# Four of ten projection units reload raw weights and are rounded again by ScalarE in the latent blocks

## The reference, cut to what matters

```python
h = _rmsnorm(x, norm_mix_g) * (1.0 + sc1) + sh1
proj = jnp.einsum('btd,dc->btc', h, w_in)          # d = 1024, c = 2592
q, k, v, r, zf, zb, ga, gg = jnp.split(proj, [...], axis=-1)
gf = jax.nn.log_sigmoid((zf @ w_decay_f + b_decay_f)) / GATE_TAU
u = ga * jax.nn.sigmoid(gg)                        # then a 31-tap depthwise convolution
```

## Time and profile before

| | |
|---|---|
| Time before, median of 3 runs | 2376.88 us (2376.43 to 2378.6) |
| The profiled execution's own time | 2378.99 us |
| Its span, first to last instruction | 2377.3 us |
| Mean granted TensorE clock | 0.971 |
| PE busy / DVE busy / ACT busy / POOL busy | 94% / 70% / 50% / 30% |
| First stage: prompt, then blocks 0 to 3 | to about 145 us, then 145-291, 291-432, 432-572, 572-703 |

### The profile page before, as it was taken

One profiled execution on the slowest core, in us unless ns is written; L12 is line 12 of the kernel. 1 busy time (PEld: TensorE's weight loads), 2 busy tenths in 40 slices (PEclk: granted clock), 3 DMA queues, 4 the chain that ended last, 5 costly groups with the idle time before them and its releaser, 6 DMA issues.

```text
span 2377.3 us, 43867 instructions
## 1 busy us (share of the span) xinstructions
PE 2223.5 (94%) x16695; PEld 2050.0 (86%) x16695; DVE 1667.2 (70%) x2949; ACT 1195.1 (50%) x1939; POOL 704.5 (30%) x652
## 2 busy tenths in 40 slices
PE   4889999999998899976999999999999999999995
PEld 4778888898885577744999999999999999999995
DVE  2889989898898766667666656666566656666585
ACT  3765473644444455424545554455545554455573
POOL 4000000000000011101355445544555455534441
PEclk8999999999998899987999999999999999999998
DMA  8986677757847655354576677766776677766986
GB/s 297 342 312 212 232 254 242 249 199 262 241 147 232 203 197 191 106 168 117 190 210 193 183 200 200 203 197 177 202 214 192 179 200 202 203 192 184 300 251 239
DMA packets 290437, 505.79 MB, mean 213 GB/s; under 512 B 26193, under 2 KB 233934, under 8 KB 274704
## 3 DMA queue, kind: packets, MB, share of 16 engines
q1 hardware_dynamic: 250406, 376.39, 48.3%
q0 software_dynamic: 39424, 126.64, 19.6%
q10 hardware_dynamic: 490, 1.16, 0.1%
HBM read 405.61 MB, written 98.53 MB: 212 GB/s over the span
## 4 chain that ended last, share of the span: by engine, by line
PE 61%; DVE 4%; DMA 2%; ACT 1%; issue 1%; POOL 0%; SPq 0%; DVEq 0%; ACTq 0%; POOLq 0%
PE bank L1700 19%; PE bank L1702 19%; PE bank L1701 19%; PE bank L1954 1%; PE bank L2052 1%; DMA out_dram<-work_exp 1%; DVE work_exp L3063 1%; DVE work_proj L2654 1%; PE bank L1985 1%; DMA work_exp<-x_rows 0%; PE bank L2234 0%; DMA park_c<-work_proj 0%; DMA work_out<-park_c 0%; DVE work_out L2778 0%; PE bank L2061 0%
## 5 line engine op out<-in xcount | busy, mean ns | idle before, releaser
L1700 PE MATMUL bank<-act_hl_exp,hl_exp 128*128 128x288 f32 x3072 | 911.2, 297 | 11.7 <-DVE hl_exp L3242 7.7
L1701 PE MATMUL bank<-act_hl_exp,hl_exp 128*128 128x288 f32 x3072 | 908.9, 296 | 0.0
L1702 PE MATMUL bank<-act_hl_exp,hl_exp 128*128 128x288 f32 x3072 | 907.3, 295 | 0.0
L1700 PEld LDWEIGHTS bank<-act_hl_exp,hl_exp 128*128 128x128 f32 x3072 | 578.5, 188 | 12.7 <-DVE hl_exp L3242 9.2
L1702 PEld LDWEIGHTS bank<-act_hl_exp,hl_exp 128*128 128x128 f32 x3072 | 580.5, 189 | 0.0
L1701 PEld LDWEIGHTS bank<-act_hl_exp,hl_exp 128*128 128x128 f32 x3072 | 579.0, 188 | 0.0
L3242 DVE TENSOR_TENSOR hl_exp<-work_exp,hl_exp 128x1024 fp32r<-128x1024 f32 x192 | 231.4, 1227 | 206.4 <-ACT hl_exp L1283 206.4
L3242 DVE TENSOR_TENSOR hl_exp<-raw_exp,hl_exp 128x1024 fp32r<-128x1024 f32 x192 | 232.1, 1225 | 193.0 <-ACT hl_exp L1283 193.0
L2654 DVE SCALAR_TENSOR_TENSOR work_proj<-work_proj,wcv 128x392 f32<-128x392 f32 (+12 forms) x600 | 338.9, 635 | 1.2
L1283 ACT ACTIVATE hl_exp<-work_exp 128x1024 fp32r<-128x1024 f32 x192 | 199.3, 1055 | 201.3 <-PE bank L1702 201.1
L1283 ACT ACTIVATE hl_exp<-raw_exp 128x1024 fp32r<-128x1024 f32 x192 | 198.5, 1052 | 161.2 <-PE bank L1702 161.2
(11 more groups left out here) (425 smaller groups left out, 3288.8 us busy)
## 6 DMA issues: line engine op xcount, KB each, us to landing
hl_proj<-park_w POOLq DMA_DIRECT2D x80, 1024.0 KB, 6.4
raw_exp<-in_w_e_gate_dram SPq DMA_DIRECT2D x32, 1024.0 KB, 5.9
raw_exp<-in_w_e_up_dram SPq DMA_DIRECT2D x32, 1024.0 KB, 5.9
work_exp<-in_w_e_gate_dram SPq DMA_DIRECT2D x32, 1024.0 KB
work_exp<-in_w_e_up_dram SPq DMA_DIRECT2D x32, 1024.0 KB, 6.0
raw_exp<-in_w_e_down_dram SPq DMA_DIRECT2D x32, 1024.0 KB, 6.0
work_exp<-in_w_e_down_dram SPq DMA_DIRECT2D x32, 1024.0 KB, 6.1
park_w<-hl_proj SPq DMA_DIRECT2D x8, 2048.0 KB, 12.2
```

Source lines behind the costliest of these rows:

```text
L1700: pe.matmul(out, lh, rh, start=first, stop=False)
L1701: pe.matmul(out, lh, rl, start=False, stop=False)
L1702: return pe.matmul(out, ll, rh, start=False, stop=last_)
```

## The change

For units 2, 3, 4 and 5 (`ROUNDED`), three things change.

- The prompt stores only their low parts: 1 MB instead of 2 MB for each.
- In latent blocks POOL issues two transfers for each half: the raw weights (512 KB) from `w_in` into the place of the high part, and the low part (512 KB) from `park_w`. Both count on the same semaphore. A row of `w_in` has 2592 columns, so the raw half comes in runs of 128 floats (512 bytes), eight for each partition.
- ScalarE waits for both transfers, rounds the raw half in place (`round_half`, 128x1024) and raises `s_rnd`, and TensorE waits for `s_rnd` instead of the load. There are 8 such instructions in each latent block, 32 in all.

```diff
+        ROUNDED = (2, 3, 4, 5)
...
                     if j + 2 < NPROJ:
                         load_proj(j + 2)
-                    if SLOT[j] < 2:
+                    if j not in ROUNDED:
                         sp.dma_start(park_w[j], hl[:, SLOT[j]].bitcast(f32)).then_inc(s_stored[SLOT[j]], 16)
                         return
+                    if SLOT[j] < 2:
+                        sp.dma_start(park_w[j, :, :, 1], hl[:, SLOT[j], :, 1].bitcast(f32)).then_inc(s_stored[SLOT[j]], 16)
+                        return
                     for q in range(2):
-                        for i in range(2):
-                            sp.dma_start(park_w[j, :, q, i], w_part(b, j, q, i).bitcast(f32)).then_inc(s_wst2, 16)
+                        sp.dma_start(park_w[j, :, q, 1], w_part(b, j, q, 1).bitcast(f32)).then_inc(s_wst2, 16)
...
+            def round_half(b, j, q):
+
+                if b.prompt:
+                    return
+                b.wait(act, s_w[j % 2][q], loads_in(j))
+                act.activation(hl[:, j % 2, q, 0], hl[:, j % 2, q, 0].bitcast(f32), ACT.Copy).then_inc(s_rnd.sem, 1)
...
+                round_half(b, 2, 0)
                 sigmoid(b, 1, 0)
...
                 act.activation(W2["B"][:, 0:H * T], W2["B"][:, 0:H * T], ACT.Ln, bias=1.0).then_inc(s_ln.sem, 1)
+                round_half(b, 2, 1)
                 sigmoid(b, 1, 1)
                 proj_hi(b, 3)
                 for q in range(2):
                     copies(b, 2, q, "k", 1.0, s_kfb)
+                    round_half(b, 3, q)
...
                 for q in range(2):
                     copies(b, 3, q, "q", DK ** -0.5, s_qfb)
+                round_half(b, 5, 0)
...
             def load_w(b, j, q):
+                if j in ROUNDED:
+                    o = PROJ_COLS[j] + 128 * q
+                    pool.dma_start(hl[:, j % 2, q, 0], w_in_v[:, :, o:o + 128]).then_inc(s_w[j % 2][q].sem, 16)
+                    pool.dma_start(hl[:, j % 2, q, 1], park_w[j, :, q, 1]).then_inc(s_w[j % 2][q].sem, 16)
+                    return
                 pool.dma_start(hl[:, j % 2, q], park_w[j, :, q]).then_inc(s_w[j % 2][q].sem, 16)
...
                 if b.prompt:
                     pe.wait_ge(s_lo[s], 2 * (j // 2) + q + 1)
+                elif j in ROUNDED:
+                    b.wait(pe, s_rnd, 2 * (j - ROUNDED[0]) + q + 1)
                 else:
-                    b.wait(pe, s_w[s][q], 16 * (j // 2 + 1))
+                    b.wait(pe, s_w[s][q], loads_in(j))
```

More of the change, by code:

```diff
@@ L358, in hybrid_layer @@
         s_wst = [sem("s_wst0"), sem("s_wst1")]
-        s_w = [[sig(f"s_w{i}{q}", 0, 16 * (NPROJ // 2)) for q in range(2)] for i in range(2)]
+        s_w = [[sig(f"s_w{i}{q}", 0, 16 * (NPROJ // 2 + 2)) for q in range(2)] for i in range(2)]
         s_uh = sig("s_uh", 2 * NPROJ + 1, 2 * NPROJ + 1)
@@ L402, in hybrid_layer @@
         r_lt, r_co = s_pf.again(0), s_pb.again(0)
+        s_rnd = Sig(s_col, 0, 8, 2)
         r_wo = [Sig(s_m1[i], 0, 0, 16) for i in range(4)]
@@ L445, in hybrid_layer @@
         s_stored = [*s_wst, s_wst2]
-        f_x = [Sig(s_wst2, 0, 0, 16 * 8), Sig(sem("f_x1"), 0), Sig(k_T, 0, 0, 2), Sig(k_e, 0, 0, 1)]
+        f_x = [Sig(s_wst2, 0, 0, 16 * 4), Sig(sem("f_x1"), 0), Sig(k_T, 0, 0, 2), Sig(k_e, 0, 0, 1)]
         f_st = [Sig(s_vec2, 0, 0, 16), Sig(sem("f_st1"), 0)]
@@ L495, in turn, with loads_in @@
             return (base + j) // 2 + (per // 2) * i if not isinstance(i, int) or i else (base + j) // 2
-        SLOT, SLOT_TURN = (0, 1, 2, 0, 1, 2, 0, 1, 0, 1), (1, 1, 4, 2, 2, 8, 3, 3, 4, 4)
+        SLOT, SLOT_TURN = (0, 1, 2, 0, 1, 2, 0, 1, 0, 1), (1, 1, 2, 2, 2, 4, 3, 3, 4, 4)
+        ROUNDED = (2, 3, 4, 5)
+        def loads_in(j):
+            return 16 * sum(2 if i in ROUNDED else 1 for i in range(j % 2, j + 1, 2))
         SLOT_BEFORE = {j: max(i for i in range(j) if SLOT[i] == SLOT[j]) for j in range(3, NPROJ)}
@@ L958, in stage2 @@
                     modulate(nb, 0)
+                    round_half(b, 4, 0)
+                    round_half(b, 4, 1)
                 b.wait(act, s_cum, 2)
@@ L964, in stage2 @@
                                ACT.Exp, scale=1.0 / TAU).then_inc(s_D.sem, 1)
+                if b.i > 0:
+                    round_half(b, 4, 0)
                 b.wait(act, s_cl, 3)
@@ L1004, in latent_rest @@
                     modulate(nb, 1)
+                round_half(b, 5, 1)
+                if nb is not None:
                     modulate(nb, 2)
@@ L1726, in value_half @@
                 elif q == 0:
-                    b.wait(pe, s_w[s][0], 16 * (j // 2 + 1))
-                    b.wait(pe, s_w[s][1], 16 * (j // 2 + 1))
+                    b.wait(pe, s_w[s][0], loads_in(j))
+                    b.wait(pe, s_w[s][1], loads_in(j))
                 value_tile(b, j, 2 * q)
@@ L1850, in latent_rest @@
                     mod_pair(b, 0)
-                b.wait(pe, s_w[0][0], 16 * 5)
+                b.wait(pe, s_w[0][0], loads_in(8))
                 b.wait(pe, s_v, 1)
@@ L1857, in latent_rest @@
                 proj_part(b, 8, 0, 4, KC, 0, b.T).then_inc(s_uh.sem, 1)
-                b.wait(pe, s_w[0][1], 16 * 5)
+                b.wait(pe, s_w[0][1], loads_in(8))
                 b.wait(pe, s_v, 3)
@@ L1862, in latent_rest @@
                 proj_part(b, 8, 1, 4, KC, 0, b.T).then_inc(s_uh.sem, 1)
-                b.wait(pe, s_w[1][0], 16 * 5)
+                b.wait(pe, s_w[1][0], loads_in(9))
                 b.wait(pe, s_v, 2)
@@ L1870, in latent_rest @@
                     mod_pair(b, 1)
-                b.wait(pe, s_w[1][1], 16 * 5)
+                b.wait(pe, s_w[1][1], loads_in(9))
                 b.wait(pe, s_v, 4)
```

## The result

| | before | after |
|---|---|---|
| Time, median of 20 runs of each | 2378.16 us (2376.43 to 2381.5) | 2384.48 us (2379.28 to 2387.09) |
| Ratio of the times | | 1.0026, 95% interval 1.002 to 1.0032 |
| Span of the profiled execution | 2377.3 us | 2384.5 us |

The ratio says that the change makes the kernel 6.2 us slower, 4.8 to 7.6 us by its interval, a little beyond the 0.2% that was called no change. The forecast was 3.5 us, and 1 to 6 us as its own range, so 6.2 lies just outside that. The time itself, 2384.48 us, is 4.1 us above the 2380.4 forecast, and 1.3 us of that is the median of before, which came out at 2378.16 instead of 2376.88. The direction and most of the places were right, and the size was not.

A forecast was written before the change was run, and what follows sets the result against it. TensorE, busy 94% of the span, was taken as the bound, prompt transfers as hidden. Block 0, blocks 1 and 2, block 3, prompt: 1.7 + 1.8 + 0 - 0 = 3.5 us on 2376.9 gave 2380.4 us, range 2374.5 to 2385.5.

The forecast's parts named there:

- Prompt, 0: Prompt: 4.19 MB less stored, 10.9 us of transfer time, hides behind VectorE and ScalarE and gains 0.
- No load late, roundings of 1.05 us: Latent blocks: pairs land in 7.5 us, within about 10 us, costing 0; each ScalarE rounding takes 1.05 us.
- rival A: Latent blocks: pairs land late, or a stall costs clock; slower by over 0.2%, 11.6 us, 2388.5 us; chance 0.18.
- The estimate of 8.4 us: Landing of a pair of loads in latent blocks by the skill's rule: 6.4 + 2.0 us, still inside 10.4 us.
- Half (2, 1) in blocks 1 and 2, 0.91 each: Sigmoid of (1, 1) 2.1 us late against 1.19 us slack: PE stalls 0.91 us per block, together 1.8 us.
- Block 0, 1.7: Block 0: PE stalls of 0.37 us at (2, 1) and 1.49 us at (5, 0), together 1.86; taken as 1.7.
- The wait at (5, 0): Block 0: PE waits 1.49 us for ScalarE's rounding of (5, 0), late behind the copies of unit 3.
- Block 3, 0: Block 3: a PE wait swallows the first rounding, the sigmoid of (1, 1) is 1.05 us late within slack; cost 0.
- the milder form of rival A: Block 0: the clock falls behind the 1.5 us stall, adding 1.7 us; no separate chance given.

The follow-up runs named there:

- run 3: The changed kernel, but the prompt stores both parts of all ten units again, 4.19 MB more: 2385.43 us against 2377.3 before, ratio 1.0032.
- run 9: The changed kernel with the low-part stores of units 2 to 5 cut to an eighth each: block 0 starts at 145.47 us; no total time given.
- run 4: The changed kernel with the roundings of (2, 0), (2, 1) and (5, 0) moved to other places on ScalarE: 2381.5 us against 2377.3 before, ratio 1.002.
- run 1: The changed kernel with its smaller stores and pairs of loads but without the 32 roundings: 2379.13 us against 2377.3 before, ratio 1.0005.
- run 6: The changed kernel, but both halves of unit 2 are rounded twice: 2394.82 us against 2376.66 before, ratio 1.0078.
- run 2: The kernel before, with its full stores and whole loads, plus the 8 roundings in each latent block: 2383.61 us against 2377.3, ratio 1.0026.
- run 7: The changed kernel with full stores and both halves of each pair loaded from park_w in 4 KB runs: 2383.21 us against 2376.66 before, ratio 1.0027.

## Why the forecast was right in kind and too small

The forecast is 2.7 us too small, and block 3, put at nothing, is most of that.

- **Prompt, 0:** right. The saved 4.2 MB are worth nothing that can be told from the spread (runs 3 and 9).
- **No load late, roundings of 1.05 us:** right, but by luck in part. ScalarE has no idle time before a rounding. The halves have median landings of 5.1 and 5.5 us against 6.4 for a whole load. But I took 7.5 us for the pair of (2, 0), from medians, and that pair took 11.2 and 11.0 us in blocks 1 and 2, and 9.3 in run 4, where 11.9 were available. Another 0.9 us, and rival A would have begun. The whole load of (2, 0) in the kernel before took 6.4, 9.3, 11.1 and 8.0 us in blocks 0 to 3; that place should have been read, and not the median of 80 loads. The estimate of 8.4 us by the Trainium skill, "DMA: Bandwidth & Descriptors", section "Anatomy of one DMA — SWDGE (gpsimd) path", was nearer, but it rests on the same median, and the 2.0 us that it adds can't be told here: in block 1 the pair took 11.2 and 9.3 us in two kernels and the whole load 9.3 us before.
- **Half (2, 1) in blocks 1 and 2, 0.91 each:** right in mechanism, too small in size. It cost 1.40 each. I took the slack as 1.19 us, from the time at which ScalarE's copies are released (323.73). PE's own row in the kernel before has the first matmul of (2, 1) earlier:

```profile
323.53 0.39 PE L1700 MATMUL bank<-act_hl_proj,hl_proj 128*128 128x512 f32 x1
```

The product was ready at 322.54, which leaves 0.99 us. The row of the engine that waits should have been used, not that of one that it releases. The sigmoid was also later than 2.1 us: from the block's start, at 35.14 instead of 32.96, 2.18 us. The product's lateness of 2.2 less 1.0 gives 1.2, and the last 0.2 us are a slower start behind the wait, with matmuls of 0.50 and 0.40 us where the flowing ones take 0.39 and begin 0.23 us apart.
- **Block 0, 1.7:** 2.4 in the first profile, 1.4 as the mean of five profiles with the change (145.53, 143.09, 145.25, 143.83, 143.77) less that of three without it (143.14, 142.39, 143.03). That mean mixes two clocks. From 80 to 100 us into the block the granted clock is 0.91 in some profiles and 1.00 in the others, whatever the kernel; at 0.91 the change costs 2.3 us (145.53 and 145.25 against 143.14 and 143.03), at 1.00 it costs 1.2 (143.09, 143.83 and 143.77 against 142.39). The wait at (5, 0) is 1.08 or 1.09 us in all five, where 1.49 was forecast. The one at (2, 1) is there in two of them only, 0.88 and 0.60 us. Not all of block 0 is ScalarE's either: run 1, at 0.91 and without a rounding, has 144.76 us.
- **Block 3, 0:** this is the step that failed: a term put at nothing. It cost 1.9 us in the first profile, 2.0 as the mean of four with the change (138.99, 137.90, 139.00, 139.21) less that of two without. ScalarE's part was right: the sigmoid of (1, 0) took up the first rounding, and (2, 1) does not wait. What I left out is that VectorE's and ScalarE's lateness also sets when the second stage's loads go out, and that the load of (6, 1) shares the DMA engines with them. SP issues the first of them 61.87 us into the block before, 62.86 in the changed kernel and 62.82 with the roundings alone. PE comes to unit 6 only 0.2 us later than before (74.77 instead of 74.57 us into the block), but the load lands 1.05 us later. The wait for (6, 1) is 2.16 and 2.84 us without the change, 3.11 with the pairs alone, 3.09 with the roundings alone (and 0.58 more for unit 7 behind it), and 3.48 to 4.13 with both, at the change's places. How it grows with the lateness is not shown: in run 6 the loads go out another 1.1 us later, and the waits are 2.86 us and 0.52 for unit 7.

Behind these waits the clock falls, the milder form of rival A at another place than the one I looked at. The changed kernel's first profile:

```profile
650.00:655.00 5.00, 3.15 (x15) 3.19 (x16) 4.85 (x10) 0.00 (x0) 0.00 (x0) 0.53 1.17 339
```

The same 20 us of block 3 (75 to 95 us from its start) before, in the changed kernel's first and second profile, and with the roundings alone (granted clock third from the end):

```profile
643.49:663.49 20.00, 17.59 (x140) 17.36 (x141) 19.56 (x35) 1.43 (x3) 0.00 (x0) 0.91 0.73 217
```

```profile
648.39:668.39 20.00, 16.54 (x118) 16.57 (x119) 19.85 (x35) 1.20 (x2) 0.00 (x0) 0.83 0.74 224
```

```profile
646.54:666.54 20.00, 16.78 (x132) 16.68 (x134) 19.85 (x35) 1.20 (x2) 0.00 (x0) 0.91 0.76 227
```

```profile
646.28:666.28 20.00, 16.59 (x142) 16.19 (x143) 19.85 (x35) 1.69 (x3) 0.00 (x0) 1.00 0.70 220
```

At the same 0.91 the changed kernel's block 3 is 0.8 and 1.5 us longer than in the two profiles of before (137.90 against 137.10 and 136.43), and its wait is 0.6 and 1.3 us longer: there the wait is nearly all of it. The three profiles with the change at 0.83 take another 1.2 us, with waits only 0.3 us longer on average. And run 2's block 3 of 136.84 us, which seemed to show that the roundings cost nothing there, kept the clock at 1.00. In the kernel before 15 matmuls from 647.44 us on begin 0.21 us apart instead of 0.12, so that fall costs some 1.4 us (an estimate); run 2 did not pay it, and it has the longer waits.

The sum of these means, 1.4 + 1.4 + 1.4 + 2.0 = 6.2 us, meets the ratio's 6.2. It is not proof of each term, since blocks 0 and 3 depend on the clock of the few executions that have a profile, and run 4 keeps 4.8 us without the two stalls. How often the clock falls in an execution, and in which block, stays open, and with it how the medians divide between wait and clock.

## What to carry to other kernels

A transfer that is saved beside a saturated queue is worth only what someone waits for it, and here a third of the queue's work in the prompt could go without TensorE starting block 0 any earlier. A small piece of work on an idle engine costs what it is late ahead of the tightest consumer: look for the one place with under 2 us of slack (here one unit of four), measure the slack on the waiting engine's own rows, and leave that unit out. Follow lateness through to transfers issued by an engine that is late, since DMA engines that are full there turned 1 us of lateness into 2. And read a load's landing at the place that matters, not as a median over all places.

## What the runs showed of the hardware

- A wait of PE can cost more than its length: 1.40 us for one shown as 1.08. Behind waits of 3.26 and 3.27 us the granted clock was 0.71 over 5 us in one case and 1.00 in the other, at the same place of two blocks, for a price of 1.6 us between them.
- Loading the raw half of each pair in eight runs of 512 bytes in each partition, instead of one of 4 KB, raised the DMA share from 0.62 to 0.84 at 182 and 189 GB/s (runs 7 and 3). The Trainium skill, "DMA: Bandwidth & Descriptors", section "Why small descriptors are slow (HBM only)", has a fixed overhead for each packet; the trace agrees in direction.
- VectorE ran slower beside POOL's issue of such a load. Its scaling of the next rows (128x1024), in the kernel with the pairs, and with the pairs contiguous (min, median and max in ns):

```profile
L2492 DVE TENSOR_SCALAR work_proj<-work_proj,stat x12: 735/743/1137, 160.9 to 451.3; 128x1024 f32<-128x1024 f32 x12
```

```profile
L2489 DVE TENSOR_SCALAR work_proj<-work_proj,stat x12: 745/749/754, 161.4 to 449.6; 128x1024 f32<-128x1024 f32 x12
```

Four of them take 3.04 us from 307.53 us on, while POOL issues the loads of (2, 1), and 2.74 us in the kernel before. These 0.3 us stand ahead of Abs, and they are the difference between stalls of 1.08 us with short runs (changed kernel, run 3) and 0.78 us without them (runs 2 and 7). The Trainium skill, "GPSIMD Engine Reference", section "Specifications", says that POOL's SBUF interfaces are shared with VectorE, and names contention for a VectorE instruction in a 2-port perf mode or with two SBUF inputs; whether this scaling is of that kind, and whether that is the reason here, was not tested.
